# Last 22 bits of a threshold search shared by ScalarE and the vector engine, and the extraction rounds moved between stages

## The chip, the core and the metric

The kernel runs on one core of one Trainium2 chip. The metric is the device time of one execution in microseconds (us); before the change it is 1909.49 us, the median of three runs (1908.1 to 1911.69). One more execution was profiled; all rows below are from it. Engines in the rows: PE is TensorE's matmuls, PEld its weight loads, DVE the vector engine, ACT ScalarE, POOL GpSimd, SP the engine that issues most DMAs. L868 is line 868 of the kernel.

## The reference

One inference step of a two-layer trunk. Layer 0 is sparse attention: an indexer scores every admissible key of every query, the 256 best keys of each query are attended to. A prompt of 1024 tokens and 64 sample rows (8 sequences of 8 tokens with 8192 cached keys each) go through it. Layer 1 is a gated DeltaNet. All arithmetic is float32. What the change touches is the choice of keys:

```python
def _indexer_topk(iq, iw, ik, q_pos, topk):
    s = jnp.einsum('bthd,bld->bthl', iq, ik)
    score = jnp.einsum('bth,bthl->btl', iw, jax.nn.relu(s))
    score = jnp.where(jnp.arange(L)[None, None, :] <= q_pos[None, :, None], score, -jnp.inf)
    _, idx = lax.top_k(score, topk)          # topk = 256
    return idx, idx <= q_pos[None, :, None]
```

The outputs are the layers' results for prompt and samples, the new keys and values, the indexer's keys, and DeltaNet's states.

## The kernel before

The program is a series of stages, each a block in which every engine has its own instruction list; between two stages all engines meet at a barrier. In the order of time: index_project (projections of the indexer, scores of the prompt), sample_scores (scores of the sample rows against the cache), head_project (q, k, v and gate of layer 0), prompt_attend, dn_inputs (norm, z and gates of layer 1), conv_attend (layer 1's convolution inputs, with the attention of the sample rows beside them), dn_sample and dn_scan (the delta rule).

Two long jobs of the vector engine have no stage of their own and are spread over the stages of others.

The first is the **search** of the prompt's thresholds. A block is 128 queries, on the 128 partitions; block i has (i+1)*128 scores in `key_mask`. Blocks 0 and 1 need no search. Blocks 2, 3 are one group, blocks 4 to 7 (640, 768, 896 and 1024 wide, the wide blocks) the other (`GROUPS`). A step for bit k counts in each block how many scores are at or above the candidate `bs_cand` (L117, one instruction a block), rejects or keeps the bit (L134), and writes the next candidate (L136). After 32 bits come four `choose` steps, which turn the scores of a block into a mask and settle ties by position. `TOPK_IN` says which steps run in which stage: steps 44 to 53 of the list (bits 10 to 19 of the wide blocks) at the start of head_project, one more after two norms, the other 11 bits and the four choose steps spread over the rest of the stage.

The second is the **extraction** of the 256 best of the sample rows' scores (`scores`, 128 partitions x 4100): 32 times a maximum of eight (L1065), its indices (L1067) and their replacement (L1069), so 96 rounds (`NX`), one instruction each. `NX_P` = 31 of them run in head_project, the next 40 (to `NX_B` = 71) in prompt_attend, the last 25 in dn_inputs. `merged()` and `page_rows` (L1613 to L1663) follow there and turn them into page rows for the gathers of conv_attend.

In **head_project** TensorE multiplies 8 blocks of 128 rows (n = 1 to 8) and the 64 sample rows (n = 0) by five chunks of weights each (c = 0 to 4); a chunk of a block is 16 matmul rows of the profile. Six PSUM banks (`ACC`) hold chunks. ScalarE takes them out (`take`, `gate`), squares the heads (`squares`, L950), and evacuates transposes (`evac`); GpSimd makes the reciprocal roots; the vector engine multiplies them in (`norms(n)`, L1015), after which TensorE transposes (`turn`, L881). `turn(0, 0)` stands behind chunk (1, 3), and `norms(0)` ahead of it on the vector engine stands behind ten bits of the search. Each engine's order is the order of the code; `between` puts extraction rounds at fixed places.

In **dn_inputs** TensorE transposes block n+1 (L1541, after `norm(n+1)`, L1636, of the vector engine) and multiplies block n in two halves (L1555). Between the norms stand 25 rounds, in front of and behind each. GpSimd makes the gated z of each block (L1530) and the reciprocal root for a norm (L1519).

## Time and profile before

| | us |
|---|---|
| median of three runs | 1909.49 |
| profiled execution, its own time | 1912.06 |
| its span | 1909.9 |
| PE busy | 1784.1 (93%) |
| DVE busy | 1290.0 (68%) |
| ACT busy | 664.8 (35%) |
| POOL busy | 516.5 (27%) |
| mean granted clock of TensorE, share of full speed | 0.966 |

The span is the stretch between the first and the last instruction in the profile. Busy time is a sum over one engine's instructions; a matmul's end is modelled, so the shares say where an engine has gaps rather than how well it is used. A row of the timeline holds one or several like instructions: start, duration, engine, line, operation, output and input, shape, how many, and in brackets how long the engine stood idle before it and what released it. The distance between two starts is the better measure of a cost where instructions overlap.

### The profile page before, as it was taken

How to read it: one execution, taken by the hardware profiler on the slowest of the kernel's cores; microseconds unless marked ns; L12 is line 12 of the kernel's file. 1: busy time of each engine (PE TensorE's matmuls, PEld its weight loads, DVE VectorE, ACT ScalarE, POOL GpSimd, SP SyncE). 2: the span in 40 equal slices, each digit the busy share in tenths (PEclk: the TensorE clock that was granted, in tenths of full speed). 3: DMA queues.
4: the chain of work that ended last, by engine and by line, in shares of the span. 5: the costliest groups of instructions: out<-in, count | busy, mean ns of one | idle time of the engine just before them, and what ended most of it. 6: DMA issues, size and time to landing. Idle time of an engine off the chain costs nothing. (4 is left out here: it accounts for less than half of the span.)

```text
span 1909.9 us, 26618 instructions
## 1 busy us (share of the span) xinstructions
PE 1784.1 (93%) x10165; PEld 1023.9 (54%) x10165; DVE 1290.0 (68%) x2099; ACT 664.8 (35%) x1625; POOL 516.5 (27%) x584
## 2 busy tenths in 40 slices
PE   6898999999989999999999999999987879999997
PEld 5553434444445566664444544444434877777674
DVE  1389999889956799986998343333443666776671
ACT  3337841211224343331211322222112545654550
POOL 2121300100101111000113777777602402222220
PEclk9999999999999999999999999999998879999998
DMA  4124530110124122103122455555668445343220
GB/s 132 36 91 156 197 135 14 39 44 28 51 100 191 63 70 98 36 12 102 67 68 67 133 166 167 167 145 167 203 223 314 114 140 151 91 109 82 76 65 33
DMA packets 159445, 207.36 MB, mean 109 GB/s; under 512 B 45160, under 2 KB 109120, under 8 KB 159296
## 3 DMA queue, kind: packets, MB, share of 16 engines
q1 hardware_dynamic: 117336, 149.65, 24.0%
q0 software_dynamic: 16896, 50.35, 8.3%
q10 hardware_dynamic: 25088, 5.66, 1.5%
q8 instruction: 82, 1.34, 0.3%
q14 instruction: 43, 0.35, 0.1%
HBM read 161.89 MB, written 43.74 MB: 108 GB/s over the span
## 5 line engine op out<-in xcount | busy, mean ns | idle before, releaser
L1962 PE MATMUL acc_ch<-xnT,w_ch 128*128 128x512 f32 x736 | 329.3, 596 | 0.6 <-ACT x_pad L1995 0.6
L1962 PEld LDWEIGHTS acc_ch<-xnT,w_ch 128*128 128x128 f32 x736 | 134.5, 190 | 153.1 <-issue 152.5
L868 PE MATMUL acc<-w_qg,xnT 128*128 128x512 f32 x384 | 170.8, 598 | 0.0
L1831 POOL DMA_INDIRECT kg<-in_cache_k,rowidx x128 | 132.1, 1032 | 38.9 <-issue 37.0
L1065 DVE MAX8 top_v<-scores 128x8 f32<-128x4100 f32 x32 | 141.7, 4429 | 0.7
L1067 DVE FIND_INDEX8 top_i<-top_v,scores 128x8 uint32<-128x4100 f32 x32 | 141.5, 4423 | 0.0
L1069 DVE MATCH_REPLACE8 scores<-top_v,scores 128x4100 f32<-128x4100 f32 x32 | 141.3, 4414 | 0.0
L1838 POOL DMA_INDIRECT home<-in_cache_v,rowidx x128 | 130.3, 1018 | 39.0 <-issue 38.4
L3010 PE MATMUL PY<-home,ogT_dn 128*128 128x512 f32 x288 | 134.5, 613 | 1.8 <-DVE y_t L3487 0.9
L1266 PE MATMUL ring<-w_out_att,ogT_blk 128*128 128x512 f32 x256 | 113.3, 601 | 7.2 <-DVE nmx_blk L1347 4.5
L868 PEld LDWEIGHTS acc<-w_qg,xnT 128*128 128x128 f32 x384 | 71.7, 192 | 82.7 <-issue 82.7
L868 PE MATMUL acc<-w_kvq,xnT 128*128 128x512 f32 x256 | 111.4, 593 | 0.0
L1995 ACT COPY x_pad<-acc_ch 128x512 f32<-128x512 f32 x48 | 28.0, 586 | 203.5 <-PE acc_ch L1962 196.5
L117 DVE TENSOR_SCALAR_CACHE_REDUCE junk_topk_h<-key_mask,bs_cand 128x640 f32<-128x640 f32 (+1 forms) x92 | 95.6, 1077 | 2.1 <-PEq L557 0.6
L2072 DVE SCALAR_TENSOR_TENSOR y_ch<-x_pad,conv_w,y_ch 128x1024 f32<-128x1024 f32 x72 | 92.5, 1285 | 2.6
L1347 DVE CUSTOM_DVE_ANT_0 lm<-ring,key_mask,q_scale 128x128 f32<-128x128 f32 (+7 forms) x64 | 51.7, 815 | 54.0 <-PE ring L1227 50.2
L2080 DVE SCALAR_TENSOR_TENSOR y_ch<-th_ch,y_ch 128x1024 f32<-128x1024 f32 x24 | 29.5, 1229 | 85.4 <-ACT th_ch L2004 85.4
L2070 DVE TENSOR_SCALAR y_ch<-x_pad,conv_w 128x1024 f32<-128x1024 f32 x24 | 19.5, 813 | 99.8 <-ACT x_pad L1995 99.8
L1299 ACT COPY pT_blk<-tp_blk 128x512 f32<-128x512 f32 (+3 forms) x96 | 43.1, 486 | 124.1 <-PE tp_blk L1236 123.9
L1266 PEld LDWEIGHTS ring<-w_out_att,ogT_blk 128*128 128x128 f32 x256 | 48.7, 192 | 68.9 <-issue 61.8
L1227 PE MATMUL ring<-kT,w_kvq 128*128 128x512 f32 (+3 forms) x192 | 74.8, 501 | 11.6 <-PEq L718 5.9
L3010 PEld LDWEIGHTS PY<-home,ogT_dn 128*128 128x128 f32 x288 | 53.7, 196 | 58.9 <-issue 57.5
(468 smaller groups left out, 3231.5 us busy)
## 6 DMA issues: line engine op xcount, KB each, us to landing
w_ch<-in_dn_w_in SPq DMA_DIRECT2D x24, 512.0 KB, 5.1
qkv_d<-y_ch SPq DMA_DIRECT2D x24, 512.0 KB, 6.5
qkv_t<-qkv_d SPq DMA_DIRECT2D x8, 1536.0 KB, 8.1
home<-in_dn_w_in SPq DMA_DIRECT2D x5, 2048.0 KB, 12.1
x<-in_x_all SPq DMA_DIRECT2D x9, 512.0 KB, 4.0
out_y_all<-y_t SPq DMA_DIRECT2D x9, 512.0 KB, 2.9
w_kvq<-in_att_w_in SPq DMA_DIRECT2D x2, 2048.0 KB, 11.1
w_qg<-in_att_w_in SPq DMA_DIRECT2D x2, 2048.0 KB, 16.4
```

The lines of the kernel that those rows point to most:

```text
L117: ins = dve.tensor_scalar(junk[:, a:a + w], block(i), thr(s), 0.0, op, ALU.add, accum_out=cnt[:, s:s + 1])
L868: ins = pe.matmul(acc[rows(n), k % ACC, :], xnT[:, kk, cols(n)], w[:, kk, :], start=(kk == 0), stop=(kk == KT - 1))
L1065: link(dve.max(v, scores[:]))
L1067: dve.max_index(top_i[:, 8 * r:8 * r + 8], v, scores[:])
L1069: link(dve.match_replace(scores[:], v, scores[:], -3e38))
L1227: ins = pe.matmul(dst[:, a:a + w], q[:, i % 2, h, :], kT[:, h // GRP, a:a + w], start=True, stop=True)
L1266: ins = pe.matmul(dst[:, a:a + 512], ogT[:, h, :], wo[:, h, a:a + 512], start=(h == 0), stop=(h == H - 1))
L1831: pool.indirect_dma_start(kg[:, j % KR, c, :], None, ck, bass.IndirectOffsetOnAxis(ap=rowidx[:, c, query(j):query(j) + 1], axis=0)).then_i ...
L1838: pool.indirect_dma_start(vg[:, j % VR, c, :], None, cv, bass.IndirectOffsetOnAxis(ap=rowidx[:, c, query(j):query(j) + 1], axis=0)).then_i ...
L1962: ins = pe.matmul(acc[:, s, :], w[:, c % WR, k, :], xT[:, k, s * 512:(s + 1) * 512], start=(k == 0), stop=(k == KT - 1))
L2072: ins = dve.scalar_tensor_tensor(out, src, tap, out, ALU.mult, ALU.add)
L3010: ins = pe.matmul(PY[:], ogT[:, h, :], wo[:, h, r * 512:(r + 1) * 512], start=(h == 0), stop=(h == H - 1))
```

## The change

`TOPK_IN["heads"]` now holds only the four choose steps. Bits 10 to 31 of the wide blocks go through a new class. For each of these 22 bits, `sign` lets ScalarE sum the signs of (candidate - score) of blocks 6 and 7, `below` lets the vector engine count scores below the candidate in blocks 4 and 5, and `settle` compares all four sums with limits, rejects or keeps the bit and writes the next candidate. `settle` waits for ScalarE (`sums_ok`), the next `sign` and `below` for it (`cand_ok`). `finish` corrects a candidate where scores equal to it were counted as halves. On ScalarE the 22 `sign` calls stand between the takes of the chunks, the last behind chunk (4, 2). On the vector engine each bit is followed by one extraction round; the norms stand at fixed bits; the four choose steps come at n = 5 to 8 with three and two rounds beside them. `NX_P` is 40 and `NX_B` 80: 40 rounds in head_project, again 40 in prompt_attend, 16 in dn_inputs, there three behind each norm. The wait for the gains' DMAs (`const_in`) and their scaling stay ahead of the norms, and with the search behind them they are now the first of the vector engine's work in the stage.

```diff
@@ -45,9 +45,10 @@
 ATT_IN = 3144
 GROUPS = ((2, 3), (4, 5, 6, 7))
 SEARCH = [(group, k) for group in GROUPS for k in range(32 + len(group))]
-TOPK_IN = {"index": (0, 4), "index_late": (4, 15), "sample_scores": (15, 44), "heads": (44, 54), "heads_gate": (54, 55), "heads_late": (55, len(SEARCH))}
+TOPK_IN = {"index": (0, 4), "index_late": (4, 15), "sample_scores": (15, 44), "heads": (34 + 32, len(SEARCH))}
+SIGN_FROM = 44 - 34
 NX = 3 * TOPK // 8
-NX_P, NX_B = 31, 71
+NX_P, NX_B = 40, 80
 NX_C = 0
 WR = 3
...
+class SignSearch:
...
+    def block(self, i):
+        return self.keep["key_mask"][:, KM[i]:KM[i + 1]]
+
+    def sign(self, act, k):
+        if k > SIGN_FROM:
+            act.wait_ge(self.cand_ok, k - SIGN_FROM)
+        a = 0
+        for s, i in list(enumerate(self.group))[2:]:
+            w = (i + 1) * P
+            if s == 3:
+                ins.then_inc(self.sums_ok, 1)
+                act.wait_ge(self.sums_ok, 2 * (k - SIGN_FROM) + 1)
+            ins = act.activation(self.junk[:, 0:w], self.block(i), ACT.Sign, bias=self.cand[:, s:s + 1].bitcast(F32), scale=-1.0,
+                                 accum_out=self.sums[:, s:s + 1])
+        ins.then_inc(self.sums_ok, 1)
+
+    def below(self, dve, link, k):
+        if k > SIGN_FROM:
+            dve.wait_ge(self.cand_ok, k - SIGN_FROM)
+        for s, i in list(enumerate(self.group))[:2]:
+            w = (i + 1) * P
+            ins = dve.tensor_scalar(self.junk[:, 1024:1024 + w], self.block(i), self.cand[:, s:s + 1].bitcast(F32), 0.0, ALU.is_lt, ALU.add,
+                                    accum_out=self.sums[:, s:s + 1])
+            link(ins)
+
+    def settle(self, dve, link, k):
+        b = 31 - k
+        dve.wait_ge(self.sums_ok, 2 * (k - SIGN_FROM) + 2)
+        link(dve.tensor_tensor(self.late[:], self.sums[:], self.limit[:], ALU.is_gt))
+        link(dve.tensor_scalar(self.rej[:], self.late[:], 0.5, float(1 << b), ALU.is_gt, ALU.mult))
+        dve.scalar_tensor_tensor(self.cand[:], self.cand[:], 1 << (b - 1) if b else 0, self.rej[:], ALU.bitwise_xor, ALU.bitwise_xor).then_inc(self.cand_ok, 1)
+
+    def finish(self, dve, link):
+        c, t, n = self.cand[:].bitcast(F32), self.late[:], self.nxt[:]
+        dve.wait_ge(self.cand_ok, 32 - SIGN_FROM)
+        link(dve.scalar_tensor_tensor(t, c, -1.0, c, ALU.mult, ALU.max))
+        link(dve.scalar_tensor_tensor(n, t, 0.6 * 2.0 ** -23, c, ALU.mult, ALU.add))
+        a = 0
+        for s, i in enumerate(self.group):
+            w = (i + 1) * P
+            if s == 3:
+                link(ins)
+                a = 0
+            ins = dve.tensor_scalar(self.junk[:, a:a + w], self.block(i), n[:, s:s + 1], 0.0, ALU.is_ge, ALU.add, accum_out=self.cnt[:, s:s + 1])
+            a += w
+        link(ins)
+        link(dve.tensor_tensor(t, n, c, ALU.subtract))
+        link(dve.scalar_tensor_tensor(t, self.cnt[:], float(TOPK), t, ALU.is_ge, ALU.mult))
+        link(dve.tensor_tensor(c, c, t, ALU.add))
 def index_project(nc, env):
+        sums_ok, cand_ok, limit_ok = sem("sums_ok"), sem("cand_ok"), sem("limit_ok")
+        search = SignSearch(keep, GROUPS[1], junk, sums, late, limit, nxt, sums_ok, cand_ok)
         st = [env["stores"][f"st{u}"] for u in range(2)]
         NST = 4
@@ -776,6 +843,9 @@
         @block.gpsimd
         def _(pool):
             link = chain(pool, pool_chain)
+            for c, i in enumerate(GROUPS[1]):
+                ins = pool.memset(limit[:, c:c + 1], float((i + 1) * P - (1 if c < 2 else 2) * TOPK))
+            ins.then_inc(limit_ok, 1)
             link(pool.memset(mhalf[:], -0.5))
             def rms_heads(n):
@@ -973,17 +1043,31 @@
                     dst = kTn[:] if n == 0 else kT[:, :, (n - 1) * P:n * P]
                     ins = act.copy(dst, src[:, 0:2, :])
                 ins.then_inc(tp_evac, 1)
+            bits = iter(range(SIGN_FROM, 32))
+
+            def sign():
+                k = next(bits, None)
+                if k is not None:
+                    search.sign(act, k)
+            sign()
             take_samples(0)
+            sign()
             take(1, 0)
+            sign()
             take(1, 1)
+            sign()
             take_samples(1)
             squares(0)
+            sign()
             take(1, 2)
             squares(1)
+            sign()
             gate_samples()
+            sign()
             for c in (3, 4):
                 gate(1, c)
                 evac(0, c - 3)
+                sign()
             evac(0, 2)
             for n in range(2, m):
                 for c in range(NC):
@@ -995,13 +1079,14 @@
                         evac(n - 1, c - 1)
                     if c == 2:
                         squares(n)
+                    sign()
             for u in range(3):
                 evac(m - 1, u)
         @block.vector
         def _(dve):
-            topk = prompt_topk(keep, junk, dve, env["topk_chain"]["link"])
-            topk(*TOPK_IN["heads"])
+            toplink = env["topk_chain"]["link"]
+            topk, first = prompt_topk(keep, junk, dve, toplink), TOPK_IN["heads"][0]
             dve.wait_ge(const_in, 48)
             dve.tensor_scalar(gqc[:], gqc[:], HD ** -0.5, None, ALU.mult)
             dve.tensor_scalar(gqs[:], gq[:], HD ** -0.5, None, ALU.mult).then_inc(gains_ok, 1)
@@ -1015,27 +1100,33 @@
                     ins = dve.scalar_tensor_tensor(r, r, rsh[q, par, h:h + 1], (gqs if h < H else gk)[q, :], ALU.mult, ALU.mult)
                 ins.then_inc(nat_ok, 1)
-            norms(0)
-            norms(1)
-            topk(*TOPK_IN["heads_gate"])
-            parts, (u0, u1) = 2 * (m - 3) + 1, TOPK_IN["heads_late"]
-            share = [1 if SEARCH[n][1] < 32 else 2 for n in range(u0, u1)] + [1] * NX_P
-            due = [max(0, int(sum(share[:n]) * (parts + 0.5) / sum(share) - 0.5)) for n in range(len(share))]
-
-            def beside(k):
-
-                search = [u0 + n for n in range(u1 - u0) if due[n] == k]
-                rounds = [n for n in range(NX_P) if due[u1 - u0 + n] == k]
-                if search:
-                    topk(search[0], search[-1] + 1)
-                if rounds:
-                    between(dve, rounds[0], rounds[-1] + 1)
-            for n in range(2, m):
-                k = 2 * (n - 2)
-                beside(k)
+            turn = [0]
+
+            def rounds(count):
+                between(dve, turn[0], turn[0] + count)
+                turn[0] += count
+
+            dve.wait_ge(limit_ok, 1)
+            for k in range(SIGN_FROM, 32):
+                search.below(dve, toplink, k)
+                search.settle(dve, toplink, k)
+                if k == SIGN_FROM + 5:
+                    norms(0)
+                elif k == SIGN_FROM + 7:
+                    norms(1)
+                n, c = divmod(k - SIGN_FROM - 9, NC)
+                if n >= 0 and c == 3:
+                    norms(n + 2)
+                rounds(1)
+            search.finish(dve, toplink)
+            norms(4)
+            for n in range(5, m):
+                topk(first + n - 5, first + n - 4)
+                rounds(3)
                 norms(n)
                 if n < m - 1:
-                    beside(k + 1)
+                    rounds(2)
+            rounds(NX_P - turn[0])
 def selection_homes(home):
@@ -1634,19 +1725,10 @@
             def norm(n):
                 dve.wait_ge(rs_ok, n + 1)
                 dve.scalar_tensor_tensor(x[n % XR], x[n % XR], rs[:, n % 2, :], gx, ALU.mult, ALU.mult).then_inc(xn_ok, 1)
-            def rounds(k):
-                a, e = (NX_B + (NX - NX_B) * q // (2 * NB - 2) for q in (k, k + 1))
-                between(dve, a, e)
-
-            for n in range(NB):
-                if n < NB - 1:
-                    rounds(2 * n)
-                if n + 2 < NB:
-                    norm(n + 2)
-                if n < NB - 1:
-                    rounds(2 * n + 1)
-                else:
-                    merged()
+            for n in range(2, NB):
+                norm(n)
+                between(dve, *(min(NX, NX_B + 3 * q) for q in (n - 2, n - 1)))
```

On the vector engine, from the start of head_project; `junk_topk_h` is the search's scratch, `bs_cand` the candidate, `scores` belongs to the extraction. Before (the first rows of ten bits, and the last):

```order
L117 TENSOR_SCALAR junk_topk_h,bs_cnt<-key_mask,bs_cand 128x640 [waits topk_chain]
L117 TENSOR_SCALAR junk_topk_h,bs_cnt<-key_mask,bs_cand 128x768
L117 TENSOR_SCALAR junk_topk_h,bs_cnt<-key_mask,bs_cand 128x896
L117 TENSOR_SCALAR junk_topk_h,bs_cnt<-key_mask,bs_cand 128x1024 [waits topk_chain]
L134 TENSOR_SCALAR bs_rej<-bs_cnt 128x4 [waits topk_chain]
L136 SCALAR_TENSOR_TENSOR bs_cand<-bs_cand,bs_rej 128x4 [waits topk_chain]
...
L1006 TENSOR_SCALAR gq_col<-gq_col 128x1 [waits hp_const_in,topk_chain]
L1007 TENSOR_SCALAR gqs<-gq 128x128
L1015 SCALAR_TENSOR_TENSOR raw<-raw,rsh,gqs 64x128 [waits hp_rsh_ok,hp_gains_ok]
```

The same place now, to the first round, and the end of the sixth bit:

```order
L1091 TENSOR_SCALAR gq_col<-gq_col 128x1 [waits hp_const_in]
L1092 TENSOR_SCALAR gqs<-gq 128x128
L195 TENSOR_SCALAR junk_topk_h,sign_sums<-key_mask,bs_cand 128x640 [waits hp_limit_ok,hp_gains_ok]
L195 TENSOR_SCALAR junk_topk_h,sign_sums<-key_mask,bs_cand 128x768 [waits topk_chain]
L202 TENSOR_TENSOR too_high<-sign_sums,sign_limit 128x4 [waits hp_sums_ok,topk_chain]
L203 TENSOR_SCALAR bs_rej<-too_high 128x4 [waits topk_chain]
L204 SCALAR_TENSOR_TENSOR bs_cand<-bs_cand,bs_rej 128x4 [waits topk_chain]
L1156 MAX top_v<-scores 128x8
...
L204 SCALAR_TENSOR_TENSOR bs_cand<-bs_cand,bs_rej 128x4 [waits topk_chain]
L1100 SCALAR_TENSOR_TENSOR raw<-raw,rsh,gqs 64x128 [waits hp_rsh_ok]
```

The wait for the gains' DMAs moved from behind ten bits to the front; the first norm moved from behind ten bits of four counts to behind six bits of two counts and five rounds.

On ScalarE, around the only load of a function table in head_project (`sgate` is the gate of the sample rows). Before:

```order
L950 ACTIVATE sq,ssh<-raw 128x128 x10
L938 ACT_TABLE_LOAD
L938 ACTIVATE sgate<-acc 128x512
L958 ACTIVATE sgate<-acc 128x512
L971 COPY qTb<-tpb 128x4x64
```

Now:

```order
L1020 ACTIVATE sq,ssh<-raw 128x128 x10
L186 ACTIVATE junk_topk_h,sign_sums<-key_mask,bs_cand 128x896
L186 ACTIVATE junk_topk_h,sign_sums<-key_mask,bs_cand 128x1024
L1008 ACT_TABLE_LOAD
L1008 ACTIVATE sgate<-acc 128x512
L186 ACTIVATE junk_topk_h,sign_sums<-key_mask,bs_cand 128x896
L186 ACTIVATE junk_topk_h,sign_sums<-key_mask,bs_cand 128x1024
L1028 ACTIVATE sgate<-acc 128x512
L1041 COPY qTb<-tpb 128x4x64
```

Two activations for each bit came between the takes; the table load stays one.

On the vector engine in dn_inputs, from the norm of block 5 to that of block 6 (the fourth and fifth in the stage). Before:

```order
L1636 SCALAR_TENSOR_TENSOR x_dn<-x_dn,dn_rs,dn_ahead 128x1024 [waits drs_ok]
L1069 MATCH_REPLACE scores<-top_v,scores 128x4100
L1065 MAX top_v<-scores 128x8 [waits extract]
L1067 MAX_INDEX top_i<-top_v,scores 128x8 [waits extract]
L1069 MATCH_REPLACE scores<-top_v,scores 128x4100
L1636 SCALAR_TENSOR_TENSOR dn_ahead<-dn_ahead,dn_rs 128x1024 [waits drs_ok,extract]
```

Now:

```order
L1727 SCALAR_TENSOR_TENSOR x_dn<-x_dn,dn_rs,dn_ahead 128x1024 [waits drs_ok]
L1160 MATCH_REPLACE scores<-top_v,scores 128x4100
L1156 MAX top_v<-scores 128x8 [waits extract]
L1158 MAX_INDEX top_i<-top_v,scores 128x8 [waits extract]
L1727 SCALAR_TENSOR_TENSOR dn_ahead<-dn_ahead,dn_rs 128x1024 [waits drs_ok]
```

One round less stands between these two; between the norms of blocks 2 and 3 three stand instead of four.

## Rows read from the trace of the kernel before

**Rows 1.** Busy time by stage: stretch, its length, each engine's busy us, PEclk, DMA, GB/s
```profile
314.30:570.70 256.40, 250.07 (x647) 114.54 (x646) 212.57 (x198) 54.95 (x209) 17.05 (x21) 1.00 0.14 50
...
1021.30:1422.80 401.50, 398.64 (x1600) 188.58 (x1600) 170.50 (x232) 98.20 (x180) 267.44 (x259) 1.00 0.54 166
```
**Rows 2.** PE's waits from 250 to 1030 us: total us, times, longest
```profile
PE acc_ch L1541 <- DVE dn_ahead L1636: 4.2, 1, 4.2
...
PE tpb L881 <- DVE raw L1015: 2.2, 1, 2.2
```
**Rows 3.** Timeline of PE, head_project
```profile
305.13 0.46 PE L881 MATMUL tpb<-ident,raw 64*128 64x64 f32 x4 [2.18 <-DVE raw L1015]
305.52 8.83 PE L868 MATMUL acc<-w_qg,xnT 128*128 128x512 f32 x16
```
**Rows 4.** Timeline of DVE, head_project
```profile
302.37 2.18 DVE L1015 SCALAR_TENSOR_TENSOR raw<-raw,rsh,gqs 64x128 f32<-64x128 f32 x8
...
305.52 0.87 DVE L117 TENSOR_SCALAR_CACHE_REDUCE junk_topk_h<-key_mask,bs_cand 128x640 f32<-128x640 f32 x1
...
306.32 1.00 DVE L117 TENSOR_SCALAR_CACHE_REDUCE junk_topk_h<-key_mask,bs_cand 128x768 f32<-128x768 f32 x1
...
308.44 1.28 DVE L117 TENSOR_SCALAR_CACHE_REDUCE junk_topk_h<-key_mask,bs_cand 128x1024 f32<-128x1024 f32 x1
...
309.76 0.17 DVE L134 TENSOR_SCALAR bs_rej<-bs_cnt 128x4 int32<-128x4 f32 x1
```
**Rows 5.** Timeline of ACT, head_project's start: issue of a DMA
```profile
256.56 0.59 ACTq L905 DMA_DIRECT2D gq_col<-in_att_q_gain  x1
```
**Rows 6.** The tile gq_col: from the issue to the landing
```profile
DMA to landing us min/median/max: 7.7/7.7/7.7
```
**Rows 7.** Timeline of ACT, dn_inputs
```profile
881.51 1.06 ACT L1583 ACTIVATE junk_dn<-x_dn 128x1024 f32<-128x1024 f32 x1
882.47 0.19 ACT L1583 ACTIVATION_READ_ACCUMULATOR junk_dn<-x_dn 128x1 f32 x1
```
**Rows 8.** Timeline of ACT, head_project: chunk c = 0 of two blocks
```profile
499.13 0.37 ACT L915 COPY v_nat<-acc 128x256 f32<-128x256 f32 x1 [6.27 <-PE acc L868]
...
534.56 0.37 ACT L915 COPY v_nat<-acc 128x256 f32<-128x256 f32 x1 [6.27 <-PE acc L868]
```
**Rows 9.** Timeline of DVE, dn_inputs
```profile
936.40 1.26 DVE L1636 SCALAR_TENSOR_TENSOR x_dn<-x_dn,dn_rs,dn_ahead 128x1024 f32<-128x1024 f32 x1
...
942.10 4.43 DVE L1065 MAX8 top_v<-scores 128x8 f32<-128x4100 f32 x1
946.57 0.09 DVE L1067 MATCH_VALUE_LOAD top_i<-top_v,scores 128x8 f32 x1
...
950.99 0.07 DVE L1069 MATCH_VALUE_LOAD scores<-top_v,scores 128x8 f32 x1
...
955.49 3.04 DVE L1636 SCALAR_TENSOR_TENSOR dn_ahead<-dn_ahead,dn_rs 128x1024 f32<-128x1024 f32 x1
```
**Rows 10.** Timeline of PE, dn_inputs
```profile
939.63 1.04 PE L1541 MATMUL acc_ch<-ident,x_dn 128*128 128x128 f32 x8
...
947.38 7.03 PE L1555 MATMUL acc_dn<-home,xnT 128*128 128x512 f32 x16
958.59 1.97 PE L1541 MATMUL acc_ch<-ident,dn_ahead 128*128 128x128 f32 x8 [4.19 <-DVE dn_ahead L1636]
...
967.98 7.03 PE L1555 MATMUL acc_dn<-home,xnT 128*128 128x512 f32 x16
```
**Rows 11.** Timeline of POOL, dn_inputs
```profile
943.25 0.54 POOL L1519 TENSOR_TENSOR dn_rs<-dn_ss,mhalf_dn 128x1 f32<-128x1 f32 x1
955.12 2.34 POOL L1530 TENSOR_TENSOR gz<-tanh_z,gain_o 128x1024 f32<-128x1024 f32 x1 [11.33 <-ACT tanh_z L1599]
```
**Rows 12.** Timeline of DVE, end of dn_inputs
```profile
1017.71 0.43 DVE L1663 TENSOR_TENSOR home<-scores 128x256 f32<-128x256 f32 x1
```
**Rows 13.** Timeline of PE, end of dn_inputs
```profile
1014.06 7.03 PE L1572 MATMUL acc_ch<-xnT,w_ch 128*128 128x512 f32 x16
```

More of the change, by code:

```diff
@@ L158, in prompt_topk, with __init__ @@
     return run
+class SignSearch:
+    def __init__(self, keep, group, junk, sums, late, limit, nxt, sums_ok, cand_ok):
+        self.keep, self.group, self.junk, self.sums, self.late, self.limit, self.nxt = keep, group, junk, sums, late, limit, nxt
+        self.sums_ok, self.cand_ok = sums_ok, cand_ok
+        self.cand, self.rej, self.cnt = keep["bs_cand"], keep["bs_rej"], keep["bs_cnt"]
+    def block(self, i):
[43 more added lines that the diff above has]
+        link(dve.tensor_tensor(c, c, t, ALU.add))
@@ L738, in head_project @@
         mhalf = sb("mhalf_h", [P, H + G])
+        sums, late, limit, nxt = (sb(k, [P, 4]) for k in ("sign_sums", "too_high", "sign_limit", "next_float"))
         tpb = ctx.enter_context(nc.psum_tensor("tpb", [P, 2, 4, P], F32))
@@ L1636, in norm @@
                 dve.scalar_tensor_tensor(x[n % XR], x[n % XR], rs[:, n % 2, :], gx, ALU.mult, ALU.mult).then_inc(xn_ok, 1)
[L1637 to L1649 removed]
+            for n in range(2, NB):
+                norm(n)
+                between(dve, *(min(NX, NX_B + 3 * q) for q in (n - 2, n - 1)))
+            merged()
             page_rows(keep, sel, dve, link, 0)
```

## The prediction, made before the changed kernel ran

> **What bounds the kernel now.** I read the page first: TensorE is busy for 93% of the span, every other engine less than 70%. So time can only come from TensorE's gaps, or from work that opens new ones. Then the busy time by stage [rows 1]: in head_project from 314 to 571 us it works 250 of 256 us while the vector engine works 213 and ScalarE 55; in conv_attend 398.6 of 401.5 us. There the vector engine is not the bound, and taking counts from it buys nothing by itself. The next view is TensorE's waits [rows 2]: of those in the stages that the change touches, two are for the vector engine, 4.2 us in dn_inputs (for a norm, L1636) and 2.2 us in head_project (for the first norm, L1015). The other long ones (barriers, prompt_attend's residuals) stand where the change alters nothing: prompt_attend has 40 rounds before and after, and starts with the same kind of round, since 31 and 40 leave the same remainder by three.
>
> The timelines give what each wait really costs. In dn_inputs [rows 10] the block before goes from 939.63 to its second half at 947.38 in 7.75 us. The next starts its wait at 958.59 - 4.19 = 954.40 and reaches its second half at 967.98: 13.58 us. The surplus is 5.83 us, 4.19 of waiting and 1.64 because the transposes take 1.97 instead of 1.04 us and the first matmuls are slow too. In head_project [rows 3] TensorE is idle from 302.95 to 305.13, and the chunk behind needs 8.83 us where an undisturbed one needs 7.03 [rows 10]: 2.18 + 1.80 = 3.98 us. Behind both gaps the matmuls are slow for a few microseconds.
>
> **Part 1, dn_inputs: nine rounds fewer.** The norm of block 6 started at 955.49 [rows 9], though its reciprocal root was there at 943.25 + 0.54 = 943.79 [rows 11]: it was queued behind extraction rounds. It then took 3.04 us instead of 1.26 [rows 9], beside GpSimd's multiplication at 955.12 [rows 11]. Rounds cost, start to start, 4.47 (maximum), 4.42 (indices) and 4.50 us (replacement) [rows 9]. By the code 16 rounds stand ahead of this norm before and 12 after. Four fewer are 17.9 us, so the engine could come to it at 937.6 and waits for the root instead: start 943.8, end 945.1, nine us before TensorE asks at 954.40. The norm of block 7 comes three rounds (13.4 us) later, at about 958.5, where TensorE needs it 14.7 us after 954.40 (7.75 and one more chunk), at 969. The cycle on the vector engine is 13.39 + 1.26 = 14.65 us for TensorE's 14.7, with a lead of nine. So the whole surplus goes: **-5.8 us**. Its bounds: 4.2 if the slow start stays for another reason, 5.8 if all goes.
>
> What is late next? The stage ends at a barrier. TensorE's last chunk ends at 1014.06 + 7.03 = 1021.09 [rows 13], the vector engine at 1018.14 [rows 12]. With nine rounds left where they were only 3.0 of the 5.8 us would pass the barrier. But nine rounds are 40 us, so page_rows ends near 980. Then conv_attend is TensorE's [rows 1], and its transfers are issued relative to the stage's start. I count no further gain and no loss there.
>
> **Part 2, head_project: the cost of a bit.** Before, a bit costs on the vector engine four counts and two small instructions, from 305.52 to 309.76 [rows 4] and 0.4 more: 4.64 us. Now it counts two blocks, each waited for. A waited-for instruction costs its duration and about 0.04 us (308.44 to 309.76 for 1.28) [rows 4]: 0.91 + 1.04 = 1.95. Settling is three instructions like that of 0.17 us, 0.2 each, the last overlapping with what follows: 0.5. With a round of 4.46 a bit takes 6.9 us. TensorE's pace is five chunks in 534.56 - 499.13 = 35.43 us [rows 8], 7.09 each, one bit to a chunk. The engines nearly match; a norm of 0.6 us in five bits makes it 7.0.
>
> ScalarE's half: a 1024-wide activation with its sum takes 1.06 + 0.19 us [rows 7], the 896-wide about 0.95 + 0.19; with a hand-over between them an estimate of 2.5 us. Bounded by neighbours: 2.0 (no read of the sum waited for) and 2.9 (twice the vector engine's 1.28 and something for the hand-over). It runs from the release of the candidate, while the vector engine does its round and two counts (6.4 us), so it is covered with 3.9 us to spare. Where ScalarE squares heads first (some 3 us) the cover is nearly used up, not exceeded. If that cover is gone, the bit grows by what is missing. Behind a waiting `sign` on ScalarE stand the next take and evacuation. TensorE needs a take six chunks later and an evacuation two turns later, about two chunks (14 us). A lag of a few microseconds costs nothing. The table load stays one, as the order shows.
>
> The Trainium skill ("ScalarE: Activation LUTs", section "Rules for kernel authors") speaks against such a move: cheap elementwise functions belong on VectorE, which is up to about three times faster per element in bf16. The trace does not bear this out for these float32 counts, 1.28 us for 1024 elements on the vector engine against 1.06 + 0.19 on ScalarE. Followed, a bit with its round would cost 4.64 + 4.46 = 9.1 us, the 22 bits with rounds would run 2 us each behind TensorE's pace, and the nine rounds would not have come forward at no cost.
>
> **Part 3, the first norm.** The head's wait is for `norms(0)`. Before, it started at 302.37 and released TensorE at 305.13, 2.76 later [rows 3, 4]. Now the vector engine first waits for the gains, whose last DMA is issued at 256.56 [rows 5] and lands 7.7 us later [rows 6], at 264.3; before, this was long over when it was asked for. The two scalings and their wait take about 0.35 us, so the first count starts at 264.7. Six bits at 1.95 + 0.5 and five rounds (maximum, indices, replacement, maximum, indices: 22.3) give 264.7 + 14.7 + 22.3 = 301.7, and TensorE is released at 304.5, a wait of 1.5 instead of 2.18 us: **-0.6 us**. The slow chunk behind I leave as it is. Bounds: DMA landing and hand-overs can shift this by 1 us either way; below, all 3.98 go if the norm is done by 302.95; above, the nearest bound is one sign not covered in each of the first bits, +3.
>
> **Part 4, the rest of head_project.** Bits end behind (4, 2), near 420 us; `finish` is some 5 us, the four choose steps were paid before too, and nine more rounds cost 40 us against the 22 x (4.64 - 2.45) = 48 us that the counts give back. The engine had waits before its norms here and keeps them. It is not late for the last one. **0 us**, because TensorE stays ahead of it or meets it in time; uncovered it would be the time by which the last norm misses TensorE's last transposes.
>
> **Sum.** -5.8 - 0.6 = -6.4 us against the profiled execution's own 1912.06 us (span 1909.9 and 2.2 around it): 1905.7, span 1903.5. That execution lies 2.6 us above the median of the runs, so the forecast for the median is 1909.5 - 6.4 = **1903.1 us**. Its own range, from the bounds of the two terms (4.2 to 5.8 and -1 to +1.6): 1901 to 1906.
>
> **Rivals.**
>
> *The first norm comes in time as well.* For it: only 1.5 us are missing, and a landing earlier by that much, or shorter hand-overs, or matmuls that are not slow behind a shorter gap, would give most of 3.98 us. Against it: the sum of six bits above has no slack of that size. Time: 1909.5 - 5.8 - 4.0 = 1899.7.
>
> *The gain is spent in head_project.* The gains' DMAs land later than 264.3, or the first signs, behind ScalarE's DMA issues and takes, are not covered: the first norm moves back by 2 to 4 us, and every us of it is one of TensorE's. For it: the wait for these DMAs is now the first thing. Against it: the same DMAs stand at the same place. Time: 1909.5 - 5.8 + 3 = 1906.7. This also stands for the case in which the dn_inputs gap passes to another wait.
>
> *ScalarE and the vector engine pass the work to and fro and hold TensorE* (the slower side). Place: `sign` and `settle` in head_project. If a sign is not beside the round but behind it, because ScalarE comes to it late each time, a bit costs 6.9 + 2.5 = 9.4 us. Against TensorE's 7.09 the lag over 22 bits is 51 us; 13 of it the banks and transposes absorb, 38 hit TensorE: 1909.5 - 5.8 + 38 = 1942. It decides from (13 + 6.4) / 22 + 7.09 = 8.0 us a bit. Against it: ScalarE is idle more than three quarters of this stage [rows 1], and each sign follows a take that is done 7 us before the next.
>
> *Nothing changes*, because the norms were not what TensorE waited for. Against it: the rows name them, and the gap starts with the norm. Time 1909.5.
>
> **Chances.** Forecast 0.62, first norm in time 0.13, spent in head_project 0.13, to and fro 0.07, nothing 0.05. The runs before spread by 3.6 us, so about 0.2% (3.8 us) is what a measurement can tell from no change; faster means below 1905.7. All of the second, nearly all of the first and a fifth of the third case are: 0.78 faster. Slower is the fourth, and a little of the third: 0.07. The rest, 0.15, is the same. The range leaves out the to and fro case and parts of the others: 1899 to 1908.
>
> **What would show it.** Of the profile after: TensorE's 4.2 us wait for a norm in dn_inputs is gone, and the transposes there are all 1.04 us; the norm of block 6 starts near 943.8 less the head's gain, right behind GpSimd's root. The first norm starts at 301 to 303 us. A bit with its round is 6.9 to 7.1 us, and a pair of signs 2.3 to 2.7. TensorE has no new wait for ScalarE between 310 and 570 us. The vector engine is idle some 35 us ahead of conv_attend. It is wrong if a TensorE wait for `acc` or `tpb` of over 1 us appears behind 314 us, if the first norm starts after 304, or if a wait of the same size appears elsewhere in dn_inputs.

## The result and the profile after

| | before | changed |
|---|---|---|
| median, beside each other on one chip (5 runs each) | 1909.13 us (1904.83 to 1911.69) | 1898.08 us (1895.31 to 1902.27) |
| profiled execution, its own time | 1912.06 | 1895.61 |
| its span | 1909.9 | 1893.6 |
| DVE busy, 264 to 571 us | 261.4 | 266.6 |
| ACT busy, 264 to 571 us | 68.2 | 119.9 |
| DVE busy, 877 to 1022 us | 137.8 | 105.7 |

The ratio is 0.9945, 95% interval 0.9925 to 0.9966: 6.5 to 14 us faster. The forecast was 1903.1 us, 6.4 us faster, with a range of 1899 to 1908. The direction was right; the time fell 0.9 us below the range. Of the runs further down, one execution of e11 took 2147.55 us at a mean granted clock of 0.83 and is left out of its ratio.

Two places of the timelines carry the argument. First TensorE at the head's first norm, in the changed kernel's first profile (start, duration, engine, line, operation, shape, count, idle time before). The first row is TensorE's first chunk of the stage (L929, 32 matmul rows):

```profile
252.78 9.88 PE L929 MATMUL acc<-w_kvq,xnT 128*64 128x512 f32 x32 [1.07 <-PEq L621]
...
301.66 0.46 PE L951 MATMUL tpb<-ident,raw 64*128 64x64 f32 x4 [0.33 <-DVE raw L1100]
302.05 7.13 PE L938 MATMUL acc<-w_qg,xnT 128*128 128x512 f32 x16
```

and in a second profile of the same kernel (run e1_after_again below):

```profile
305.34 0.46 PE L951 MATMUL tpb<-ident,raw 64*128 64x64 f32 x4 [1.54 <-DVE raw L1100]
305.73 7.13 PE L938 MATMUL acc<-w_qg,xnT 128*128 128x512 f32 x16
```

Beside [rows 3] the wait is 1.54 us instead of 2.18, and the chunk behind it takes 7.13 us instead of 8.83. In the first profile the wait is only 0.33 us, because TensorE's first chunk took 9.88 us there instead of the 8.55 of the second profile: it comes to the norm 1.3 us later and waits that much less.

The vector engine in the same stage, changed kernel, first profile; this answers to [rows 4]:

```profile
261.57 0.15 DVE L1091 TENSOR_SCALAR gq_col<-gq_col 128x1 f32<-128x1 f32 x1 [9.48 <-DMA gq_col<-in_att_q_gain]
...
261.89 0.88 DVE L195 TENSOR_SCALAR_CACHE_REDUCE junk_topk_h<-key_mask,bs_cand 128x640 f32<-128x640 f32 x1
...
264.35 4.42 DVE L1156 MAX8 top_v<-scores 128x8 f32<-128x4100 f32 x1
...
268.81 0.88 DVE L195 TENSOR_SCALAR_CACHE_REDUCE junk_topk_h<-key_mask,bs_cand 128x640 f32<-128x640 f32 x1
...
298.91 2.17 DVE L1100 SCALAR_TENSOR_TENSOR raw<-raw,rsh,gqs 64x128 f32<-64x128 f32 x8
```

A bit with its round is 268.81 - 261.89 = 6.92 us. ScalarE's half of a bit, same profile:

```profile
264.47 1.04 ACT L186 ACTIVATE junk_topk_h<-key_mask,bs_cand 128x896 f32<-128x896 f32 x1 [0.55 <-DVE bs_cand L204]
265.42 0.19 ACT L186 ACTIVATION_READ_ACCUMULATOR junk_topk_h<-key_mask,bs_cand 128x1 f32 x1
265.64 1.15 ACT L186 ACTIVATE junk_topk_h<-key_mask,bs_cand 128x1024 f32<-128x1024 f32 x1
266.69 0.18 ACT L186 ACTIVATION_READ_ACCUMULATOR junk_topk_h<-key_mask,bs_cand 128x1 f32 x1
```

2.40 us from 264.47 to 266.87, while the vector engine's round runs from 264.35 to 268.77.

The second place is dn_inputs. TensorE there, changed kernel, first profile; answers to [rows 10]:

```profile
936.07 1.04 PE L1632 MATMUL acc_ch<-ident,x_dn 128*128 128x128 f32 x8
...
950.67 1.04 PE L1632 MATMUL acc_ch<-ident,dn_ahead 128*128 128x128 f32 x8
...
958.41 7.03 PE L1646 MATMUL acc_dn<-home,xnT 128*128 128x512 f32 x16
```

The transposes of block 6 start without a wait and take 1.04 us instead of 1.97, and the block's second half starts 7.74 us behind them (958.41 - 950.67), as behind the undisturbed ones of [rows 10] (7.75). The vector engine's norm for them, answering to [rows 9]:

```profile
940.26 1.27 DVE L1727 SCALAR_TENSOR_TENSOR dn_ahead<-dn_ahead,dn_rs 128x1024 f32<-128x1024 f32 x1
...
954.85 1.28 DVE L1727 SCALAR_TENSOR_TENSOR dn_ahead<-dn_ahead,dn_rs 128x1024 f32<-128x1024 f32 x1
...
978.56 0.43 DVE L1745 TENSOR_TENSOR home<-scores 128x256 f32<-128x256 f32 x1
```

The gain by stage. All lengths are between starts of TensorE's rows that every kernel has: head_project from its first chunk to its last group of transposes, prompt_attend to dn_inputs, dn_inputs to conv_attend, conv_attend to dn_sample, and from there to the last matmul:

| profile | head's first chunk | first norm: wait, chunk behind | head_project | prompt_attend | dn_inputs | conv_attend | behind |
|---|---|---|---|---|---|---|---|
| before | 8.57 | 2.18, 8.83 | 308.9 | 306.4 | 145.1 | 405.3 | 477.8 |
| changed, first | 9.88 | 0.33, 7.13 | 306.7 | 308.5 | 139.0 | 405.2 | 471.1 |
| changed, e1 | 8.55 | 1.54, 7.13 | 306.5 | 306.4 | 138.2 | 405.3 | 476.7 |
| changed, e15 | 9.55 | 0.58, 7.13 | 306.6 | 307.5 | 139.0 | 405.2 | 471.5 |
| head alone, e2 | 8.53 | 1.63, 7.13 | 306.6 | 306.3 | 144.0 | 405.2 | 474.9 |
| dn_inputs alone, e3 | 8.58 | 2.16, 8.83 | 308.9 | 306.8 | 138.3 | 405.7 | 473.3 |

Against the one profile of the kernel before, the head gives 2.2 to 2.4 us and dn_inputs about 6. prompt_attend and what lies behind conv_attend differ by 2 to 6 us between two profiles of one and the same kernel.

The head's 2.3 us belong to executions in which the first chunk takes some 8.5 us. Run e9 below is nearly the kernel before: its first norm starts 46.55 us behind the stage's first matmul, before 46.67. It had a first chunk of 9.96 us, waited 0.67 us with 7.13 behind, and took 307.1 us for the stage. By this the kernel before would take some 307.2 us in such an execution (an estimate: 307.1 and the 0.12 us of the norm), and the change gives 0.5 us there, not 2.3.

### The profile page after: what moved, and what is told of

It is laid out like the page before. It is cut to its first block and busy times, and to the rows that moved or that the text cites. A ratio compares the mean times of both kernels' runs of the same rounds, so it can differ in the third digit from the quotient of the medians.

```text
span 1893.6 us, 26687 instructions
## 1 busy us (share of the span) xinstructions
PE 1772.1 (94%) x10165; PEld 1015.7 (54%) x10165; DVE 1243.9 (66%) x2046; ACT 714.2 (38%) x1713; POOL 514.8 (27%) x588
## 5 line engine op out<-in xcount | busy, mean ns | idle before, releaser
L938 PEld LDWEIGHTS acc<-w_kvq,xnT 128*128 128x128 f32 x256 | 48.5, 190 | 61.1 <-issue 61.0
```

What stands on the lines that cost most here:

```text
L938: ins = pe.matmul(acc[rows(n), k % ACC, :], xnT[:, kk, cols(n)], w[:, kk, :], start=(kk == 0), stop=(kk == KT - 1))
```

## The experiments

Theory A: the gain is two gaps of TensorE, each with the slow matmuls behind it; ScalarE's share only frees the vector engine. Theory B: the later stages became faster too. In two of the four batches of runs, e5 to e8 and e9 to e12, every kernel took some 60 us more, the one before too (1975.1 and 1971.4 us); in the profiles of these batches conv_attend is 54 to 67 us longer. Within such a batch only ratios and the other stages' lengths are compared. The expectations of e10 to e12 count head_project from its second chunk on: 300.4 us before, and 296.4 or 296.5 us in each of the seven profiles without a wait at the first norm (e4, e5, e8, e10, e11, e12, e16). The lengths given here include the first chunk.

**The change again.** The changed kernel as it is.

> The changed kernel once more. In its first profile TensorE waited 0.33 us for the first norm of head_project, where I had worked out 1.5, and the chunk behind ran at its normal 7.13 us; the whole span was 16.3 us shorter, of which the two places of the change explain 3.6 + 6.1. Theory A (two gaps): this is what the kernel does each time, the 0.3 to 1.5 us depend on how fast TensorE's first chunk of the stage is (8.6 or 9.9 us), and the rest of the 16.3 us is scatter between executions: ratio 0.993 to 0.996, dn_inputs without a wait for a norm. Theory B (something else gains with the changed program, in the last stage): the stretch from dn_scan's first matmul to the end is again 417 us or less, as in the first profile (1472.6 to 1889.1 and the last rows), against 423 before. Theory C (the prediction's head term was right and that profile lucky): the wait for the first norm is 1.5 us and the chunk behind takes 8.8 us: ratio 0.996 to 0.997.

Measured: 1900.04 us beside 1908.63, ratio 0.9955 (0.9938 to 0.9971). The last stages took 476.7 us, not 471.1: what Theory B rests on was not there again, and the gain was.

**Each part alone.** e2 keeps dn_inputs as before, and so 31 and 40 rounds in the stages ahead:

```diff
-NX_P, NX_B = 40, 80
+NX_P, NX_B = 31, 71
...
```

> The search as changed, but 31 rounds in head_project, 40 in prompt_attend and 25 in dn_inputs, laid out there as before. The 4.2 us wait for the norm of block 6 must come back. Theory A: gain 3 to 4 us, ratio 0.998. Theory B: 3 to 4 us and some 5 more from dn_scan, ratio 0.9955. Theory C: gain 0.6 us, ratio 1.000.

Measured: 1907.38 us, ratio 0.9996 (0.9978 to 1.0013), head_project 306.6. The stage is 2.3 us shorter than before, but the whole time shows no gain: the interval reaches from 4 us faster to 2.5 us slower, so it holds both the 3 to 4 us of the expectation's Theory A and nothing. The wait in dn_inputs is back with its slow transposes (e2's timeline):

```profile
955.21 1.97 PE L1633 MATMUL acc_ch<-ident,dn_ahead 128*128 128x128 f32 x8 [4.19 <-DVE dn_ahead L1728]
```

e3 is the kernel before with only dn_inputs in another order, nine rounds more in it than in the changed kernel:

```diff
...
+            between(dve, NX_B, NX_B + 1)
+            for n in range(2, NB):
+                norm(n)
+                between(dve, NX_B + 1 + 3 * (n - 2), NX_B + 1 + 3 * (n - 1) if n < NB - 1 else NX)
+            merged()
```

> The kernel before, with only the order in dn_inputs changed: one round, then each norm ahead of three rounds, all 25 rounds still there, the last nine behind the last norm. The prediction says that the wait for the norm goes (5.8 us on TensorE) but only 3.0 us pass the barrier, because the vector engine still ends near 1018 us. Theory A: gain 2.5 to 3.5 us, ratio 0.9985, and a wait of TensorE at the barrier ahead of conv_attend of about 3 us. Rival (the barrier is not set by the vector engine): the whole 5.8 us, ratio 0.997.

Measured: 1904.2 us, ratio 0.9978 (0.9959 to 0.9996), dn_inputs 138.3 instead of 145.1. This lies between the two expectations. Its last wait, in e3's timeline, shows the barrier met late by the vector engine, 2.01 us where the changed kernel has 0.32; the vector engine ends its own work 0.5 us before TensorE goes on:

```profile
1013.79 0.42 DVE L1655 TENSOR_TENSOR home<-scores 128x256 f32<-128x256 f32 x1
...
1014.75 0.28 PE L1844 MATMUL lgt<-ident,conv_w_nat 96*128 96x96 f32 x1 [2.01 <-PEq L1435]
```

**Both orders without ScalarE.** The kernel before with e3's dn_inputs and the first norm behind nine bits instead of ten:

```diff
-"heads": (44, 54), "heads_gate": (54, 55),
+"heads": (44, 53), "heads_gate": (53, 55),
```

> The kernel before, the whole search on the vector engine and the rounds at 31, 40 and 25 as before, with two orders changed: the first norm of head_project one bit earlier (behind nine bits of ten), and in dn_inputs each norm ahead of three rounds, as in the run with that order alone. The first norm then starts at 297.7 and is done at 300.5, before TensorE asks at 302.95. Theory A (the gain is the two waits and the slow stretches behind them, and ScalarE's share buys nothing by itself): head_project gains 4.0 us, dn_inputs 4 to 6 less 1.7 us at the barrier, together 7 to 10 us, ratio 0.9948 to 0.9965, as much as the whole change. Rival (the vector engine's 40 us less work in the search is what gains): at most the 4 us measured for the order in dn_inputs, ratio 0.998.

Measured: 1967.42 beside 1975.1 us, ratio 0.9958 (0.9930 to 0.9987), head_project 303.5 (with a first chunk of 7.09 us, 1.5 less than before's), dn_inputs 138.2. Two moved orders, without a count on ScalarE, bring a gain of the change's size, within its interval of 2.6 to 14 us. The norm alone, in the kernel before (e10):

> The kernel before with the first norm of the head behind nine bits instead of ten; no work to ScalarE, and dn_inputs as before. Theory A (the head's gain is the gap at the first norm, its wait and the slow chunk behind it): TensorE doesn't wait at the first tpb transpose, the chunk behind takes 7.1 us, the head's stage is 300.4 less 3.9 = 296.5 us, ratio about 0.998. Rival (ScalarE's share of the last bits is what brings the head's gain): the stage stays at 300 us, ratio 1.000.

Measured: ratio 0.9990 (0.9967 to 1.0014), too wide to tell 0.998 from 1.000. Its timeline tells what the stage does: no wait, 7.13 us behind; head_project 306.4, for the first chunk took 10.0 us.

**The first norm one bit earlier, or later,** in the changed kernel:

```diff
-                if k == SIGN_FROM + 5:
+                if k == SIGN_FROM + 4:    # e4, e12; e6 has + 6
```

> The changed kernel with the first norm one bit earlier, behind five bits instead of six. It then starts 6.9 us earlier, near 292 us, long before TensorE asks. Theory A: at most 0.3 us better than the changed kernel where that is lucky, up to 2 to 3 us where TensorE's first chunk is fast; never a wait for the first norm. Ratio to before 0.993 to 0.995. Theory C: 3.3 us better than the changed kernel.

Measured: 1898.43 us, ratio 0.9945 (0.9924 to 0.9965); head_project 304.9, 1.6 less than in e1. The whole time is that of the changed kernel, so here too only the stage's length shows the gain.

> The changed kernel with the first norm one bit later, behind seven bits. A bit with its round is 6.9 us, so TensorE's wait for it grows from 1.5 to 8.4 us, and the chunk behind is slow again (8.8 instead of 7.1 us) if a slow chunk follows a gap of over 2 us and none of 1.6 us. Theory A: 8 to 10 us slower than the changed kernel, ratio to before 0.999 to 1.001. Rival (the slow chunk is chance): 6.9 us slower.

Measured: ratio 1.001 (0.9981 to 1.0039); head_project 316.4. The wait, in e6's timeline:

```profile
318.29 0.69 PE L951 MATMUL tpb<-ident,raw 64*128 64x64 f32 x4 [8.36 <-DVE raw L1100]
318.91 9.68 PE L938 MATMUL acc<-w_qg,xnT 128*128 128x512 f32 x16
```

**ScalarE's share taken back.** All four blocks counted by the vector engine, the rest of the changed order kept:

```diff
     def sign(self, act, k):
+        return
...
-        for s, i in list(enumerate(self.group))[:2]:
+        for s, i in enumerate(self.group):
...
-        dve.wait_ge(self.sums_ok, 2 * (k - SIGN_FROM) + 2)
...
```

> The changed kernel with all four wide blocks counted by the vector engine (ScalarE counts none), everything else in its place, 40 rounds in head_project. A bit with its round then costs about 9.2 us on the vector engine against TensorE's 7.1. The first norm starts near 315 us, a wait of some 15 us; the norm of block 4 behind the search near 477 us, where TensorE needs it near 465, another 12. Theory A: 27 us slower than the changed kernel, more with slow stretches, ratio to before 1.009 to 1.012. Rival (norms are in time anyway and only their order counts): as fast as the changed kernel, 0.995.

Measured: 2005.33 us, ratio 1.0163 (1.0114 to 1.0213). TensorE's waits from 250 to 610 us (total, times, longest):

```profile
PE tpb L949 <- DVE raw L1098: 34.0, 3, 18.6
```

head_project is 343.7, 37 us more than the changed kernel's. That is more than the 27 us expected: the three waits are 34.0 us, where 15 and 12 had been worked out, and the first is followed by a chunk of 9.5 us. So in this order ScalarE's share is needed to pay for the nine rounds that came forward; that it doesn't bring the gain itself is e5's result.

**How long a gap, how slow the chunk behind?** e9: the kernel before with the two scalings of the gains ahead of the tenth bit.

```diff
-            topk(*TOPK_IN["heads"])
+            topk(44, 53)
             ... the two scalings ...
+            topk(53, 54)
```

> The kernel before with the two scalings of the gains moved ahead of the tenth bit of the head's search; all else as before. The vector engine's first scaling of raw comes some 0.3 us earlier, so TensorE's wait at the first tpb transpose falls from 2.18 to about 1.9 us. Theory A (the gap itself makes the chunk behind it slow, and only a gap as long as before does): the sixteen matmuls behind still take 8.8 us, and the head's stage is 0.3 us shorter. Theory B (any shortening is enough, the chunk is slow for another reason than the gap's length): 7.1 us, and 2.0 us shorter. Of the whole: 0 to -2 us, ratio 0.999 to 1.000.

Measured: ratio 1.0011 (0.9986 to 1.0036). The wait was 0.67 us, because the first chunk took 9.96, and the chunk behind 7.13: the case in between wasn't met. So two kernels put the gap back into the changed one, with one comparison more right ahead of the norm (one execution each):

```diff
                 if k == SIGN_FROM + 5:
+                    toplink(dve.tensor_scalar(junk[:, 1024:1024 + 1024], keep["key_mask"][:, 0:1024], 0.0, None, ALU.is_lt))
                     norms(0)
```

(384 instead of 1024 elements in the first.)

> The changed kernel with one comparison of 384 elements more on the vector engine, into scratch that nothing reads, right ahead of the head's first norm: some 0.4 to 0.5 us. The wait at the first tpb transpose was 1.5 us where TensorE's first chunk of the stage took 8.5 us, and 0.3 where it took 9.9; so it is 2.0 here, or 0.8 behind a slow first chunk. Theory A (a gap as long as before slows the chunk behind it, whatever made it): 8.8 us behind a wait of 2.0, 7.1 behind one of 0.8. Theory B (the change itself, not the gap's length, made that chunk normal): 7.1 in either case.

Measured: wait 0.58 us behind a first chunk of 9.89, then 7.13. With such a first chunk both theories expect 7.1, so this run doesn't tell them apart.

> The changed kernel with one comparison of 1024 elements more on the vector engine, into scratch that nothing reads, right ahead of the head's first norm: some 0.8 to 1.3 us. The wait at the first tpb transpose becomes 2.4 to 2.9 us, or 1.1 to 1.6 behind a slow first chunk. Theory A (the gap's length decides): a wait over 2.1 us is followed by a chunk of 8.8 us or more, one under 1.7 by 7.1. Theory B (not the gap's length): 7.1 in either case.

Measured: the comparison took 0.73 us, a little less than expected, behind a first chunk of 8.65. So the wait is 2.14 us instead of 2.4 to 2.9: the gap of before is back, with what belongs to it (e14's timeline):

```profile
309.99 0.46 PE L951 MATMUL tpb<-ident,raw 64*128 64x64 f32 x4 [2.14 <-DVE raw L1100]
310.37 8.83 PE L938 MATMUL acc<-w_qg,xnT 128*128 128x512 f32 x16
```

head_project is 308.9 us, to a tenth what it was before. What differs between 8.83 and 7.13 is the granted clock. Twelve microseconds from the start of that chunk, first e14, then e1 (stretch, length, busy time and count of PE, PEld, DVE, ACT, POOL, clock, DMA, GB/s):

```profile
310.40:322.40 12.00, 12.00 (x30) 5.26 (x30) 11.76 (x12) 3.50 (x7) 0.00 (x0) 0.86 0.01 1
```

```profile
305.70:317.70 12.00, 12.00 (x34) 5.42 (x33) 11.76 (x12) 3.49 (x7) 0.00 (x0) 1.00 0.01 1
```

The mean of 0.86 is the upper level (2.4 GHz) with a stretch at the lower one (1.2 GHz) in it, behind 2.14 us in which TensorE did nothing; behind 1.54 us it stayed at the upper. The Trainium skill ("TensorE: Matmul & The Clock Gate", section "HAM oscillation — how this bites in real kernels") says that waits between groups of matmuls cost more than themselves in this way; this trace agrees, with 1.7 us on top of 2.14; the waits in the page's worked example, for DMAs, are longer (some 3 to 5 us).

**A better version.** prompt_attend still had 4.5 us of waits for nmx_blk, of the vector engine; e8, e11 and e16, one kernel, move six of its 40 rounds to dn_inputs, to the end of the list there, with the norm of e4 (where the expectations say nine, it is six):

```diff
-NX_P, NX_B = 40, 80
+NX_P, NX_B = 40, 74
...
-                between(dve, *(min(NX, NX_B + 3 * q) for q in (n - 2, n - 1)))
+                between(dve, NX_B + 3 * (n - 2), NX_B + 3 * (n - 1) if n < NB - 1 else NX)
```

> The version with the first norm one bit earlier, and 34 rounds in prompt_attend instead of 40; dn_inputs takes 22, the last seven behind the last norm. The vector engine, idle 33 us ahead of conv_attend in the changed kernel, is then idle some 6 us there. In prompt_attend TensorE waits 4.5 us for `nmx_blk` and 5.3 us for a residual, part of it behind rounds. If rounds cause these waits: 2 to 5 us better than the version it starts from, ratio to before 0.991 to 0.9935. If the vector engine's own masking and residual cause them: no change, 0.9945.

> The changed kernel with the first norm one bit earlier, and with nine of the later search's rounds moved out of prompt_attend into dn_inputs. Theory A: prompt_attend loses its waits for nmx_blk, 298 us instead of 304 to 306, the head's stage 296.4, dn_inputs 137 to 138, ratio to the kernel before 0.990 to 0.992. Rival: the searches moved to dn_inputs are late there, at the merged choice or the barrier, and take 3 us or more of that back: ratio 0.9935 or more.

> The changed kernel with only the first norm one bit earlier, on the same chip as the version with fewer rounds in prompt_attend, to compare with it. Theory A: head's stage 296.4 us, prompt_attend 304 to 306, dn_inputs 137 to 139, ratio 0.9935 to 0.9945, so 6 to 8 us behind the other. Rival: no difference between the two beyond 2 us.

Measured: e8 0.9918 (0.9884 to 0.9952); e11 0.9932 (0.9909 to 0.9955) beside e12's 0.9975 (0.9950 to 0.9999), prompt_attend 297.0 beside 305.0. The distance between the two is 8 us by the ratios and 5 by the medians of the executions that the ratios use, for 6 to 8 expected, but both ratios are worse than expected (0.990 to 0.992 and 0.9935 to 0.9945). From head_project on, e12's stages outside conv_attend are as long as e4's within 2 us; what is missing isn't placed. In e12's profile head_project starts only at 262.1 us, in e11's at 256.4. Then on one chip with the changed kernel:

> The changed kernel once more, on one chip with the version with fewer rounds in prompt_attend. Ratio to the kernel before 0.9945 to 0.9965; wait at the first tpb transpose 1.5 us, or 0.3 behind a slow first chunk, and 7.1 us behind it either way; prompt_attend 305 to 308, dn_inputs 138 to 139.

> The changed kernel with the first norm one bit earlier and nine rounds fewer in prompt_attend, on one chip with the changed kernel. Theory A: no wait at the first norm, head_project 1 to 2 us shorter than the changed kernel's, prompt_attend 297 to 298 us instead of 305 to 308: 7 to 10 us faster than it, ratio to the kernel before about 0.991. Rival: under 3 us between the two.

Measured: e15 1898.39 us, ratio 0.9947 (0.9928 to 0.9966); e16 1890.24 us, ratio 0.9909 (0.9876 to 0.9942), prompt_attend 297.0. The waits of prompt_attend in e15:

```profile
PE ring L1318 <- DVE w_kvq L1463: 5.2, 5, 1.7
PE ring L1357 <- DVE nmx_blk L1438: 4.5, 2, 2.7
```

and in e16, where the second is down to 0.2 us:

```profile
PE ring L1318 <- DVE w_kvq L1463: 4.8, 6, 1.2
...
PE ring L1357 <- DVE nmx_blk L1438: 0.2, 1, 0.2
```

e16 beats both kernels, the changed one by 8 us: each of its six executions is faster than each of e15's eleven (at most 1894.13 against at least 1895.51).

## Why the prediction was off, step by step

**dn_inputs, -5.8: right.** The norm of block 6 was to start at 943.8 less the stage's shift of 3.4 us (877.2 to 873.8), so 940.4: it started at 940.26. The norm of block 7: 955.1 forecast, 954.85 measured. All later transposes are 1.04 us. The stage's length depends on how it opens, in either order. Where the first sixteen transposes take 3.8 us in one go, it is 145.1 us in the old order (before, e9) and 138.9 to 139.1 in the new (six profiles); where they are faster and only the first chunk is slow (7.6 to 8.3 us), 144.0 and 144.2 (e2, e10) against 137.9 to 138.2 (e1, e11, e12). Like with like this is 6.1 and 6.0 us, for 5.8. Where nothing is slow at the opening the new order takes 136.6 (e4, e7, e8); no profile of the old one opened so. e3 and e5 opened so too and took 138.3 and 138.2: their 1.7 us more are the barrier, met with nine rounds still in the stage. There the prediction's estimate was a loss of 2.8 us (3.0 of the 5.8 would pass), so it was too dark by 1.1. The vector engine is done at 979.0 and idle for 33 us, "some 35".

**A bit, a pair of signs: right.** 6.92 us against 6.9; 2.40 against 2.5.

**The first norm's start and the wait: right.** The gains were there 8.8 us behind the stage's first matmul (forecast 9.0), the first norm started 46.0 to 46.1 behind it (forecast 46.0), the wait was 1.54 and 1.63 (forecast 1.5) where the first chunk took 8.5 us, as in the profile that the forecast was made from, and 0.33 and 0.58 where it took 9.9 and 9.55.

**The slow chunk: this step failed.** "The slow chunk behind I leave as it is", I wrote, so the term was -0.6; measured, with a first chunk of 8.5 us, it is 0.64 of waiting (2.18 less 1.54) and 1.70 of slow matmuls (8.83 less 7.13), -2.3. The surplus itself had been taken as 1.80, against the 7.03 us of a chunk in dn_inputs; in this stage an undisturbed chunk takes 7.13. I had named the possibility among the rivals ("matmuls that are not slow behind a shorter gap") with 13 in 100 and had no row for a shorter gap. The rows of all the runs: 8.83 behind waits of 2.14, 2.16 and 2.18; 9.5 to 9.7 behind 8.36 and 18.6; 7.13 behind 1.63, 1.54, 0.67, 0.58, 0.33 and none. Nothing between 1.63 and 2.14 was met. e14 is the changed kernel with one comparison more, and the slow chunk is back: what made the chunk normal in the changed kernel is the shorter wait, not its other edits. That is one execution; before and e3 are the other two with such a gap. The first chunk was alike (8.5 to 8.65 us) in these three and in e1 and e2, so it doesn't tell the two cases apart. And the term holds only in part of the executions: where the first chunk takes 9.9 us or more, the kernel before has no slow chunk either, by e9, and some 0.5 us are left to gain.

**The rest of head_project, 0: right.** In the changed kernel's profiles (the first, e1 and e15) no row of TensorE waits for a norm or for ScalarE's takes from 314 to 558 us. e7 prices the cover: without ScalarE 37 us.

**What is left.** The two terms as measured make -6.1 - 2.3 = -8.4, or 1901.1 us from the 1909.5 of the forecast, where the first chunk takes 8.5 us, and -6.1 - 0.5 = -6.6, or 1902.9 us, where it takes 9.9 or more. Both lie within the range. The three comparisons of the changed kernel gave 0.9945, 0.9955 and 0.9947, in the mean -9.7 us, and each has an interval of 3 to 4 us either way. So 1.3 to 3.1 us are over that no stage accounts for; for one comparison this is within its interval, for the three together the larger figure hardly is. The two parts alone, e2 and e3, make 0.9996 and 0.9978, some 5 us, with intervals as wide. The rest may lie behind conv_attend: there the changed kernel took 471.1, 476.7 and 471.5, the one before 477.8 and, as e9 and e10, 475.0 and 472.2. These overlap, and over all profiles it is 471.1 to 478.3 with the new search and 472.2 to 477.8 with the old. The cause, if there is one, stays open. Part of the miss is thus the size of the range: it was made of the terms' bounds, and the scatter of a comparison of five runs, some 3.5 us, was not in it.

## What to carry over

A wait of TensorE has two prices, its own length and the slow matmuls behind it, and the second comes and goes at once, here somewhere between a wait of 1.63 and one of 2.14 us: when an edit shortens a wait without removing it, give the second price its own chance in the sum rather than keep it. Before moving work to another engine, try the order alone: here two moved places in the order gave a gain of the same size within the intervals, and the other engine's share paid for work that nobody waited for. Ask of every stage which vector work stands ahead of something that TensorE waits for; six extraction rounds taken out of prompt_attend, with the norm one bit earlier, were worth nearly as much again as the whole change.

## What was not expected of the hardware

The first chunk of head_project takes 8.5 to 8.8 us in some executions, 9.5 to 10.0 in others and 7.1 in a few (the changed kernel has 8.55, 9.55 and 9.88; e4 and e12, one kernel, 8.5 and 7.1). The granted clock of that chunk in the mean was 0.71 in the first profile of the changed kernel, 0.82 in e1 and 1.00 in e12. A later wait can swallow this: in e1 and e15 head_project is 306.5 and 306.6 us, though their first chunks differ by 1.0. The stage's start itself lies between 252.6 and 262.5 us over the eighteen profiles (252.8, 256.6 and 258.0 in the changed kernel), though no edit touches what stands ahead of it. Where no wait is left the first chunk's length shows in the stage's: 303.5, 304.9 and 306.4 us with first chunks of 7.1, 8.5 and 10.0 (e12, e4, e11).

A 1024-wide comparison on the vector engine takes 1.28 us with its count accumulated and its limit read from a tile [rows 4], and 0.69 us with a constant and no count (e14). Which of the two differences makes it wasn't tried.

conv_attend took 405 us in two batches and 459 to 473 us in two others, on one of the chips in both ways. In the longer ones TensorE's granted clock is 0.94 to 0.95 instead of 0.99 to 1.00 there and it waits, in e10 for ScalarE's scores among others:

```profile
PE tpk L1881 <- ACT scores L2020: 12.3, 3, 7.6
PE acc_ch L1962 <- issue: 12.2, 14, 3.3
```

where the kernel before has 1.6 us for the first and none for the second. The kernels are the same there; the cause wasn't looked for.
